# Thirty-two bytes more for the sums of squares of a two-block transformer kernel

## The reference, cut to what matters

```python
def first_block(x, ...):
    u = rms_norm(h, g_norm_mix)
    proj = u @ w_in + b_in                      # 1024 -> some 5,400 columns
    y_m = mlstm_mixer(...)                      # 4 heads, chunks of 128 tokens
    y_n = nsa_mixer(...)                        # compressed, selected, windowed attention
    mixed = sum(sigmoid(merge) * (ys @ w_branch))
    h = h + mixed @ w_out
    f = rms_norm(h, g_norm_ffn)
    h = h + (silu(f @ w_gate) * (f @ w_up)) @ w_down      # inner width 2816
    return rms_norm(h, g_final)

def second_block(x, mem, ...):
    h = _rmsnorm(x, g_mix)
    # h @ w_in_2 feeds three branches: gated linear attention, sparse attention, memory attention
    merged = gate0 * (o_gla @ w_o_gla) + gate1 * (o_dsa @ w_o_dsa) + gate2 * (o_mem @ w_o_mem)
    x = x + merged @ w_out
    x = x + _hier_moe(_rmsnorm(x, g_ffn), ...)  # 16 experts in 4 groups, two used by a token
    return x
```

## The kernel before

| buffer | start | by 64 | by 256 |
|---|---|---|---|
| ident; x; xn | 16512; 22784; 30976 | 0 | 128; 0; 0 |
| xT_hi; xT_lo (and xT_raw) | 39168; 47360 | 0 | 0 |
| ss | 55552, 32 bytes | 0 | 0 |
| ring and w_lo; w_hi | 55584; 88352 | 32 | 32 |
| region's start (mixT_hi, gated) | 112928 | 32 | 32 |
| h_hi; h_lo; turned | 117024; 119072; the same area | 32 | 32 |
| mem, experts' slabs; memT; xgs; o_m, merged; o_d, o_g | 134176 and up | 32 | 32 |
| ysT_lo; ysT_hi | 149792; 205216 | 32 | 32; 160 |
| mixT_lo; qk; v1 | 166272; 158080; 174464 | 0 | 128; 128; 128 |
| dkT; dqT; mkT; mqT | 138272; 207904; 134176; 150560 | 32 | 32 |

## Time and profile before

### The profile page before, as it was taken

The page is one execution under the profiler, slowest core; times in us unless marked ns, Lnnn a source line. Parts: engine busy times, 40 slices in busy tenths (PEclk is TensorE's granted clock), DMA queues, the critical chain, the costliest instruction groups (busy, mean ns, idle before and its releaser), DMA issues.

```text
span 1033.2 us, 16415 instructions
## 1 busy us (share of the span) xinstructions
PE 1013.4 (98%) x6770; PEld 912.7 (88%) x6770; DVE 682.7 (66%) x1017; ACT 585.8 (57%) x859; POOL 37.5 (4%) x49
## 2 busy tenths in 40 slices
PE   6999999999999999999999999999999989999998
PEld 6998988999999999889898868999999978888886
DVE  5865757667555554684765657556455679989983
ACT  6573576655434343474675545675444568777781
POOL 4101000000000000000000001100000000000000
PEclk9999999999999999999999999999999989999999
DMA  9994443456555565654535325553565919999981
GB/s 266 259 305 125 152 136 123 132 172 213 174 201 180 188 198 172 213 173 154 163 123 163 108 98 159 167 165 127 164 197 171 326 60 330 361 363 366 362 316 41
DMA packets 167352, 203.17 MB, mean 197 GB/s; under 512 B 11303, under 2 KB 142990, under 8 KB 167278
## 3 DMA queue, kind: packets, MB, share of 16 engines
q1 hardware_dynamic: 159598, 196.01, 58.6%
q10 hardware_dynamic: 6352, 3.19, 1.2%
q0 software_dynamic: 1328, 2.92, 1.0%
HBM read 200.51 MB, written 2.63 MB: 197 GB/s over the span
## 4 chain that ended last, share of the span: by engine, by line
PE 96%; DVE 2%; DMA 1%; ACT 1%; issue 0%; POOL 0%; DVEq 0%; ACTq 0%; POOLq 0%
PE bank L616 81%; PE bank L753 1%; PE bank L809 1%; PE bank L799 1%; PE bank L3003 1%; PE bank L3070 1%; PE bank L2596 1%; PE bank L2680 1%; DMA ring<-in_w_out 1%; PE bank L2735 1%; PE bank L2697 1%; DMA x<-in_x 1%; PE bank L2905 0%; PE bank L2910 0%; PE bank L3043 0%; PE bank L823 0%
## 5 line engine op out<-in xcount | busy, mean ns | idle before, releaser
L592 DVE TENSOR_TENSOR w_lo<-ring,w_hi 128x1024 fp32r<-128x1024 f32 (+1 forms) x302 | 423.0, 1437 | 177.1 <-ACT w_hi L584 176.3
L584 ACT ACTIVATE w_hi<-ring 128x1024 fp32r<-128x1024 f32 (+1 forms) x302 | 357.5, 1225 | 182.9 <-PE bank L616 150.7
L616 PE MATMUL bank<-xT_hi,w_hi 128*128 128x256 f32 x896 | 254.7, 284 | 0.0
L616 PE MATMUL bank<-xT_lo,w_hi 128*128 128x256 f32 x896 | 251.9, 281 | 0.0
L616 PE MATMUL bank<-xT_hi,w_lo 128*128 128x256 f32 x896 | 251.8, 281 | 0.0
L616 PEld LDWEIGHTS bank<-xT_hi,w_hi 128*128 128x128 f32 x896 | 169.1, 189 | 2.5 <-issue 1.6
L616 PEld LDWEIGHTS bank<-xT_lo,w_hi 128*128 128x128 f32 x896 | 169.2, 189 | 0.8 <-issue 0.2
L616 PEld LDWEIGHTS bank<-xT_hi,w_lo 128*128 128x128 f32 x896 | 169.1, 189 | 0.0
L616 PE MATMUL bank<-w_hi,xT_hi 128*128 128x512 f32 (+1 forms) x208 | 78.2, 376 | 0.1
L616 PE MATMUL bank<-w_lo,xT_hi 128*128 128x512 f32 (+1 forms) x208 | 76.6, 368 | 0.0
L616 PE MATMUL bank<-w_hi,xT_lo 128*128 128x512 f32 (+1 forms) x208 | 76.5, 368 | 0.0
(11 more groups left out here) (541 smaller groups left out, 1821.9 us busy)
## 6 DMA issues: line engine op xcount, KB each, us to landing
ring<-in_w_in SPq DMA_DIRECT2D x54, 1024.0 KB, 5.3
ring<-in_w_down SPq DMA_DIRECT2D x31, 1024.0 KB, 7.7
ring<-in_w_gate SPq DMA_DIRECT2D x40, 512.0 KB, 5.6
ring<-in_w_up SPq DMA_DIRECT2D x40, 512.0 KB, 8.1
ring<-in_w_gate SPq DMA_DIRECT2D x11, 1024.0 KB, 5.4
ring<-in_w_up SPq DMA_DIRECT2D x11, 1024.0 KB, 5.4
ring<-in_w_out SPq DMA_DIRECT2D x8, 1024.0 KB, 5.4
ring<-in_w_mem_kv SPq DMA_DIRECT2D x8, 1024.0 KB, 5.1
```

The source lines that it names most:

```text
L584: act.activation(HIGHS[HI_SLOT[s]][:, k, :], RAWS[SLOT[s]][:, k, :], ACT.Copy).then_inc(w_hi_ready, 1)
L592: vec.tensor_tensor(LOWS[SLOT[s]][:, k, :], RAWS[SLOT[s]][:, k, :], HIGHS[HI_SLOT[s]][:, k, :].bitcast(F32), ALU.subtract).then_inc(w_lo_r ...
L616: ins = pe.matmul(dst, a, b, start=(start and j + m == 0), stop=(stop and j == len(pairs) - 1 and m == 2), **kw)
```

## The change

One line. `ss` gets 16 floats (8 * TT, with TT = 2 token tiles) instead of 8, so 64 bytes a partition instead of 32. The floats that are used stay the same. All that is allocated after it starts 32 bytes higher: ring, w_lo, w_hi, and the whole region.

```diff
@@ -169,7 +169,7 @@
     with ExitStack() as into:
         xT_raw = sb("xT_raw", [P, KT, T], into=into)
     xT_lo = sb("xT_lo", [P, KT, T], F32R)
-    ss = sb("ss", [P, 4 * TT])
+    ss = sb("ss", [P, 8 * TT])
     raw_ctx = ExitStack()
     ring = sb("ring", [P, RAW, KT, SW], into=raw_ctx)
     raw_ctx.close()
```

## The result

The kernel got faster. Its median is 1027.82 us (1027.06 to 1028.20, 4 runs) beside 1036.18 us (1034.89 to 1038.45, 4 runs) for the kernel before on the same chip, a ratio of 0.9914 with a 95% interval of 0.9901 to 0.9928. The profiled execution took 1027.06 us.

What follows compares the result with a forecast made beforehand. PE was taken to bound the kernel, with nothing hidden behind it. Terms of +4.6, +0.3, -3.0 and -0.5 us made +1.4, giving 1036.0 from the profiled execution and 1036.6 us after 0.6 for the median; range 1029 to 1042.

Steps and rivals of the forecast that it cites:

- PE bounds, other engines and DMAs give nothing: Whole kernel: PE is 96% of the path; address changes on ACT, DVE and DMA were priced at 0, keeping +1.6 us for DMA.
- Nothing is lost to the clock: Whole kernel: the 1033.2 us span ran at granted clock 0.997, the 2.4 GHz level, so no time was lost there.
- The step depends on the two addresses: PE products: equal remainders cost 1.7 to 2.4 ns a product at 256 columns and save 6.3 at 512.
- Nothing changes: Rival, chance 0.12: region, not remainder, sets the PE step, so the time stays at 1035.2 us.
- Equal at 0 costs what equal at 32 costs: PE products with both operands at remainder 0 were assumed to step like those with both at 32.
- slabs will be at 64 by 256 and xT at 0, a difference of 64: xT products with slabs: this difference was given the 256-column step of equal operands, 120.0 ns.
- the first term of the sum: xT over a slab at 256 columns: 2688 products going from 118.3 to 120.0 ns, +4.6 us.
- The gather: Experts' 512-column products, taken to step at 233.6 ns like the scatter; 72 in both together would save 0.5 us.
- anywhere from 117 to 122: Bound in ns on the mean 256-column step at a difference of 64, around the 120.0 taken.
- Slower: a difference of 64 is a third case: Rival, chance 0.22: 256-column xT steps rise to 120.0 to 122 ns, 512-column ones stay at 233; 1041.2 us.
- Faster: Rival, chance 0.21: alignment at 0 itself helps; 512-column steps fall to 226.7 ns, 256-column ones to 117.6; 1029.8 us.
- A change in rows of operands that moved together would overthrow the rule.: Test on o, merged, h and the experts' rows: they should stay to the nanosecond if differences alone count.

Runs made afterwards that it cites:

- ss160: Kernel before with `ss` at 160 bytes instead of 32, so xT stands at distance 160 from the slabs: ratio 1.0046 to the kernel before.
- ss256: Kernel before with `ss` at 256 bytes instead of 32, so xT and slabs both stand at 0 by 256: ratio 1.0012 to the kernel before.
- ss128: Kernel before with `ss` at 128 bytes instead of 32, so xT stands at distance 128 from the slabs: ratio 1.0013 to the kernel before.
- xT32_ss64: Kernel before with 32 bytes padded ahead of xT and `ss` at 64 bytes (xT at 32, slabs at 96, distance 64): 1027.53 us, ratio 0.9923.
- xT32_ss32: Kernel before with 32 bytes padded ahead of xT, `ss` still 32 bytes (xT at 32, slabs at 64, distance 32): 1036.47 us, ratio 0.9995.
- best_h128: Kernel after with o and merged also put at distance 64 from the slabs, and h moved down by 128 bytes: ratio 0.9881 to the kernel before.
- hi_only: Kernel before with 32 bytes padded ahead of w_hi, moving w_hi and the region to 64 while ring and w_lo stay: 1038.61 us, ratio 1.0022.

## Why the prediction was wrong, step by step

**PE bounds, other engines and DMAs give nothing: right.** ACT's half slab 1053 ns before and after, DVE's 1225 and 1226, the landing 5.3 us, PE full in every stage that has the products in question. No instruction changed. The start-to-start times of line 616 and the scatter hold the whole difference to within 0.5 us. "Nothing is lost to the clock" was a little too much: in the router and the start of the gather it stood at 0.50 for 6.8 us, in the kernel before and after alike.

**The step depends on the two addresses: right.** "Nothing changes" had 0.12, and with it the rule of the Trainium skill, "TensorE: Matmul & The Clock Gate", section "Step-by-step: what each phase is for", that weight and stream come through independent ports. That the change is worth nothing, which followed from it, is not borne out for this type of product: ss160 and the kernel after differ in the size of one small buffer, and their ratios to the kernel before are 1.0046 and 0.9914.

**Equal at 0 costs what equal at 32 costs: right.** It was the first of the two things that the trace did not show. ss256 has it: 119.9 and 227.4 where 120.0 and 226.7 were taken, and the ratio that follows, 1.0012, is +1.2 us.

**"slabs will be at 64 by 256 and xT at 0, a difference of 64, where the equal ones above differ by 0 ... so I take 120.0 for 64 as well": the step that failed.** It gave distance 64 the step of distance 0, as if remainders by 64 decided, where the distance counts by 256. At 64 the 256-column step is 116.3, not 120.0, which turns the first term of the sum from +4.6 into -5.5 us, 10 us in one number. The 512-column one is 229.2, not 226.7: -1.9 instead of -3.0. The gather, taken to fall with them, stayed at 233 ns (233.0 and 233.2). With the terms as measured the same sum gives -7.5, and -8.0 with h, which it had at 0; the span fell by 7.5. The bound that I wrote, "anywhere from 117 to 122", was too tight as well: it was drawn around rows at distances 0, 32 and 128, none of which has a rhythm at 113.3.

**The evidence that was used for it** was ysT_hi at distance 128 with a mean of 120.0. One product in three of those 48 steps streams ysT_lo, which stands at distance 0, so the row was a mixed one. ss128 gives 119.3 for xT at 128, near enough; the row just says nothing of 64. The trace before had no product of this type at 64 at all.

**The rivals.** "Slower: a difference of 64 is a third case" had the right mechanism and the wrong sign: it is a case of its own, and a cheaper one. "Faster" gave 1029.8 us, 0.2% from the result, for a reason that the runs reject: it held that being at a multiple of 64 helps, and xT32_ss64 has the gain without it. Its sign in the profile, a 256-column group at 284 or less with the 512-column one at 397, came half true (282 and 401).

**"A change in rows of operands that moved together would overthrow the rule."** o, merged, turned, memT and xgs stayed within 0.1 ns. xgo rose from 227.8 to 228.8, but it has 228.9 in xT32_ss32 too, where no distance changed. h fell: 228.5 to 226.7. h stands at distance 0 in both, and across the runs its step goes with the distance of xT, 228.5 with xT at 32 (two kernels), 226.7 with xT at 64 (four) and 227.6 to 228.3 elsewhere. So it does not need a change of its own distance; that the xT products just ahead of it do this is likely, by best_h128, but no run isolates it.

## What to carry to other kernels

Where PE is full and each product brings its own stationary load, the start addresses of the two operands are a tuning knob like a tile size: pad one buffer by 32 bytes at a time over 256 bytes and measure each, since the curve can't be guessed from its neighbours. An unmeasured case wants wide bounds: the nearest rows (118 to 120 ns) gave no hint of 113. Measure the parts of one operand (high and low) at mixed distances too before using them: in hi_only xT lost more than at either distance alone, and o gained. And before runs or profiles 2 us apart are compared, look at their granted clocks: 0.997 against 0.993 is worth that much here.

## What the runs showed of the hardware that was not expected

- For these fp32r products the mean step depends on the start of the streamed operand minus that of the stationary one, by 256 bytes and with its sign: 116.3 to 119.9 ns at 256 columns, 227.4 to 234.2 at 512, and xT's two shapes have their best distances at different places (64 and 0 in the table above).
- At distance 64 there are two steady rhythms, 113.3 and 117.8 ns, and in the feed-forward the one in force is inherited from the products before. By slab, xT has two at some other distances as well, but closer together: 117.3 and 118.6 at 96, 118.6 and 120.0 at 128, 116.7 and 117.8 at 224. At 192 nearly all slabs have 117.8, but two in the first block's projections have 113.3 and 113.5. At 0, 32 and 160 there is one (120.0, 118.3, 120.0), apart from the first steps of a slab.
- Plain alignment has no price of its own: at distance 64, slabs at 64 and slabs at 96 gave 1027.82 and 1027.53 us.
- A stretch at the lower clock among the experts (granted clock 0.50 for 3.4 us, products of 512 columns at 427 ns instead of 228) is in every profile at 0.993 and 0.995 and in none at 0.996 and 0.997; it comes after the router, where PE is idle in part.
- Why the distance acts is open: no run here separates one cause from another.
